# GpSimd splits the next head's weights between the low parts of the probabilities instead of ahead of them

## The chip, the cores and the metric

The kernel runs on one core of one Trainium2 chip. The metric is the device time of one launch in microseconds (us); lower is better. The core's engines are TensorE (PE; its weight loads are listed as PEld), VectorE (DVE), ScalarE (ACT), GpSimd (POOL) and SyncE (SP), which here only issues DMAs. Each engine runs its own list of instructions in order, and they wait for one another through semaphores.

## The reference, cut to what matters

The computation is two transformer blocks over 1024 tokens with width 1024. The first has three mixers side by side, of which one is a softmax attention with forget gates ("fox", 8 heads of 64), then a gated MLP. The second is a latent attention ("mla", 16 heads, 64 + 32 for queries and keys, 64 for values). Both attentions have this core for each head and each block of queries:

```
s = jnp.einsum('bqhd,bkhd->bhqk', q, k) ...          # float32 scores
s = jnp.where(mask, s, -jnp.inf)
prob = jax.nn.softmax(s, axis=-1)
outs.append(jnp.einsum('bhqk,bkhd->bqhd', prob, v))
```

ahead of which the head's q, k and v are made by matrix products with its weights.

## The kernel before, in words

**Two-part arithmetic.** Every float32 operand `a` of a product is split into `hi` (a rounded to fp32r) and `lo = a - hi`, and a product is three matmuls: hi by lo, lo by hi, hi by hi. Weights come from HBM as 173 units of 128 x 1024 (512 KB). SP loads unit u into `w_raw` as soon as unit u-2 is split (`load`, L1894). GpSimd splits it: `w_hi` (L1919, an addition of zero that rounds), then `w_lo` (L1921, a subtraction), and counts `w_split`. TensorE waits for `w_split` before it uses a unit. There are two buffers of each.

**Attention steps.** Fox and mla run the same software pipeline, one step for each head n. The first two steps are written out, the others are a loop of two. In a step TensorE first projects head n from its weights (L220), with the first two score pieces of head n-1 in the middle. Then it attends for head n-1: the scores by keys and queries are cut into 12 pieces g, of widths 512, 384, 256, 128 (g 0 to 3, first half of the queries) and 512, 512, 512, 512, 512, 384, 256, 128 (g 4 to 11, second half). In turn for each g it does:

- the value products of the high parts of piece g (`value_pe`, L622, L623; they wait for `p_hi` of g)
- the value product of the low part of piece g-1 (`value_low_pe`, L629; it waits for GpSimd's low part of g-1)
- the scores of piece g+2 (`score_pe`, L606 to L612)
- behind g 4 to 9, the score products of head n that are needed for its row maxima (`max_pe`, L652, L654, L655), in eight groups i = 0 to 7. Group 6 stands behind g = 8 and waits until DVE has reduced five groups, group 7 behind g = 9 and waits until six are reduced.

At the end of a step come nine small transposes of v (L638, L640) and one of the maxima (L660), which waits for DVE's `mx<-mx` (L717). The next step's projection stands behind it.

**ACT** makes two exponentials of each piece: `p_hi` (L668) and, in full float32, `probs` (L670). `p_hi` of g needs the low part of piece g-2 to be done, since the buffers are shared. Behind g = 6 ACT takes the logarithm and the exponential of the first half's sums (L685, L687).

**GpSimd** makes the low parts, `probs_lo = probs - p_hi` (`low_pool`, L677), 12 for a head. Its order in step n is: split the weights of head n+1 (L1919, L1921), then the 12 low parts of head n-1.

**DVE** prepares the operands of head n (in mla with L1670, `rope_x<-rope_x,rope_y`, and last L1678, `mla_q_lo<-rope_x,mla_q_hi`), reduces the maxima groups (L712), and between the fourth and the fifth of them normalizes the first half of head n-1: L698 (`newton<-ps,r`), L701 (`rec<-newton,r`), in mla also L705 (`rec<-rec,mix`), L707 (`mix<-ps,rec`). Behind the eighth it negates the maxima (L717, 128 x 8), copies v (L722, L724) and the row of maxima (L728), and normalizes the second half (L698 to L707 again). TensorE needs `mla_q_lo` of L1678 before maxima group 0.

The first step of each attention (n = 0) has no head to attend for, and behind the last step stands the attention of the last head alone. So 7 steps of fox and 15 of mla have both a split and low parts.

Of the kernel before, what the change touches and what calls it, by code (L numbers as in the profile page):

```python
# [35 lines left out]
DT = D // P  # L36
# [67 lines left out]
def build(nc, wpack, xT, pT, vecs, consts, pos, outT, f_rows):  # L104
    with ExitStack() as ctx:
# [456 lines left out]
        N_PIECES = len(PIECES)  # L562
# [80 lines left out]
        def max_pe(pe, A, n, b, i):  # L643

            q_hi, _, k_hi, _, _ = A.bufs
            r = slice(0, A.rows_max)
            bank, reduced = MAX_BANK[i]
            if reduced:
                pe.wait_ge(A.max_done, n * N_MAX + reduced)
            queries = q_hi[b][r, i * P:(i + 1) * P]  # L650
            if i >= 4:
                nc.tensor.matmul(PS[:, bank, :], queries, k_hi[b][r, 0:HALF], start=True, stop=True)  # L652
            w, c, d = max_width(i)[0], i // 4, i % 4 * P
            nc.tensor.matmul(PS[:, bank + c, 0:w], queries, k_hi[b][r, c * HALF:c * HALF + w], start=True, stop=False)  # L654
            nc.tensor.matmul(PS[:, bank + c, d:w], ident_bf[:, :], masks[:, A.mask, 0:w - d], start=False, stop=True)\  # L655
                .then_inc(A.mp_ready, 1)
# [15 lines left out]
        def low_pool(pool, A, n, g):  # L672

            off = PIECES[g][2]
            w = slice(0, HALF - off)
            pool.wait_ge(A.exp_done, n * N_PIECES + (g + 1))
            nc.gpsimd.tensor_tensor(P_lo[g % 4][:, w], Pt[g % 4][:, w], A.p_hi[g % 2][:, w].bitcast(F32), ALU.subtract)\  # L677
                .then_inc(A.p_lo_done, 1)
# [160 lines left out]
        def steps(eng, A, step):  # L839

            for b in range(2):
                step(b, b, 0)
            with eng.Fori(1, A.heads // 2) as turn:
                for b in range(2):
                    step(turn * 2 + b, b, turn)
# [144 lines left out]
        def fox_constants_pool(pool):  # L990

            pool.wait_ge(f_stored, 32)
            pool.wait_ge(rope_s, ROPE_STEPS)
            q_hi, q_lo, k_hi, k_lo, vaug = fox.bufs
            pool.wait_ge(w_split, U_FQK + 1 + 2)
            n = 0
            for b in range(2):
                for dst, value in ((q_hi[b][HD:HD + 2, :], 1.0), (q_lo[b][HD:HD + 2, :], 0.0), (k_hi[b][HD:HD + 2, :], 1.0),
                                   (k_lo[b][HD:HD + 2, :], 0.0), (vaug[b][:, :, HD:P], 1.0)):
                    nc.gpsimd.memset(dst.bitcast(F32), value).then_inc(fox.setup, 1)  # L1000
                    n += 1
                    pool.wait_ge(fox.setup, n)
# [623 lines left out]
        def mla_constants_pool(pool):  # L1626

            pool.wait_ge(unit_done, U_Z + DT + 2)
            NKV.wait(pool, "lo", 2)
            q_hi, q_lo, k_hi, k_lo, vaug = mla.bufs  # L1630
            pool.wait_ge(w_split, U_HEAD + 1 + 2)
            n = 0
            for b in range(2):
                for dst, value in ((q_lo[b][96:97, :], 0.0), (k_hi[b][96:97, :], 1.0), (k_lo[b][96:97, :], 0.0), (vaug[b][:, :, HD:P], 1.0)):
                    nc.gpsimd.memset(dst.bitcast(F32), value).then_inc(mla_constants, 1)
                    n += 1
                    pool.wait_ge(mla_constants, n)
# [247 lines left out]
        @block.sync  # L1885
        def _(sp):
            sp.dma_start(stage[:, :], consts).then_inc(consts_in, 16)
            sp.dma_start(vec[:, :], vecs).then_inc(vecs_in, 16)
            sp.wait_ge(x_in[3], 16)
            sp.dma_start(pos_i[:, :], pos).then_inc(pos_in, 16)  # L1890

            def load(u, s):
                sp.wait_ge(w_split, u + 1)
                sp.dma_start(raw[s][:, :, :].rearrange("p k n -> p (k n)"), wpack[u, :, :] if isinstance(u, int) else  # L1894
                             wpack[bass.ds(u, 1), :, :].rearrange("o p n -> (o p) n")).then_inc(w_loaded[s], 16)
            with sp.Fori(0, N_UNITS // 2) as it:
                for s in range(2):
                    load(it * 2 + s, s)
            if N_UNITS % 2:
                load(N_UNITS - 1, 0)  # L1900
            for half in range(2):
                for i in range(DT // 2):
                    N5.wait(sp, "h", half * DT + 2 * i + 2)
                    k = 2 * i
                    sp.dma_start(outT[k * P:(k + 2) * P, cols(half)].rearrange("(k p) t -> p k t", p=P), result[:, k:k + 2, cols(half)])\
                        .then_inc(out_stored, 16)
            sp.wait_ge(out_stored, 16 * DT)

        @block.gpsimd
        def _(pool):  # L1910
            pool.sem_inc(w_split, 2)
            nc.gpsimd.memset(zero[:, :], 0.0).then_inc(zero_set, 1)
            pool.wait_ge(zero_set, 1)
            no_change = zero[:, :].rearrange("p (a n) -> p a n", a=1).to_broadcast([P, DT, P])

            def split(u, s, loads, kts=slice(0, DT)):
                pool.wait_ge(w_loaded[s], loads)
                pool.wait_ge(unit_done, u + 1)
                nc.gpsimd.tensor_tensor(w_hi[s][:, kts, :], raw[s][:, kts, :], no_change[:, kts, :], ALU.add).then_inc(w_hi_done, 1)  # L1919
                pool.wait_ge(w_hi_done, u + 1)  # L1920
                nc.gpsimd.tensor_tensor(w_lo[s][:, kts, :], raw[s][:, kts, :], w_hi[s][:, kts, :].bitcast(F32), ALU.subtract)\  # L1921
                    .then_inc(w_split, 1)

            def units(first, end, kts=DT):

                k = slice(0, kts)
                with pool.Fori(0, (end - first) // 2) as it:
                    for j in range(2):
                        split(it * 2 + (first + j), (first + j) % 2, it * 16 + ((first + j) // 2 * 16 + 16), k)
                if (end - first) % 2:  # L1930
                    split(end - 1, (end - 1) % 2, (end - 1) // 2 * 16 + 16, k)

            def heads(A, first):

                def step(n, b, turn):
                    u = first + b + 1
                    split(turn * 2 + u, u % 2, turn * 16 + (u // 2 * 16 + 16))
                    if not (isinstance(n, int) and n == 0):
                        for g in range(N_PIECES):
                            low_pool(pool, A, n - 1, g)  # L1940
                steps(pool, A, step)
                for g in range(N_PIECES):
                    low_pool(pool, A, A.heads - 1, g)
            units(0, U_FQK + 1)
            fox_constants_pool(pool)
            heads(fox, U_FQK)
            units(U_FQK + FOX_H + 1, U_DN[-1])
            units(U_DN[-1], U_MIN, MLP_CHUNKS[-1])
            units(U_MIN, U_HEAD + 1)
            mla_constants_pool(pool)  # L1950
            heads(mla, U_HEAD)
            units(U_HEAD + MLA_H + 1, N_UNITS)
# [230 lines left out]
```

## Time and profile before

| what | value |
|---|---|
| median of 3 runs | 2255.83 us (2255.39 to 2258.79) |
| profiled execution | 2258.68 us, of which the profile's span is 2256.9 us |
| busy shares of the span | PE 93%, PEld 74%, DVE 49%, ACT 29%, POOL 48% |
| TensorE's mean granted clock | 0.968 of full |
| fox steps | from about 118 to 332 us, about 30.6 us each |
| mla steps | from about 1570 to 1990 us, about 27.4 and 28.0 us each in turn |

The times are microseconds from the start of the span. A step is counted here from one L717 to the next. Where the profile gives a releaser, it is the last of the things that an instruction waited for.

### The profile page before, as it was taken

To read this page: it belongs to the slowest core of one execution; us is meant where nothing else is said; L and a number is where in the kernel's file an instruction comes from. 1 tells how busy PE (TensorE), PEld (TensorE's weight loads), DVE (VectorE), ACT (ScalarE), POOL (GpSimd) and SP (SyncE) were. 2 spreads that over 40 slices of the span, in tenths; PEclk is the share of its full clock that TensorE was granted. 3 is DMA by queue.
4 is the path that set the end of the run, shared out by engine and by line. 5 is a ranking of instruction groups with operands and counts; after the bars stand their busy time and mean duration, and the time that the engine had idled before them with its cause. 6 is when DMAs were issued, how large, how long until landed. Compare 5 with 4: busy or idle time off the path is not lost.

```text
span 2256.9 us, 27160 instructions
## 1 busy us (share of the span) xinstructions
PE 2105.2 (93%) x9840; PEld 1680.7 (74%) x9840; DVE 1111.7 (49%) x1213; ACT 661.7 (29%) x1069; POOL 1090.6 (48%) x657
## 2 busy tenths in 40 slices
PE   4999999988999999999999998997999999979996
PEld 3777777877778878888878876886777777758774
DVE  6545553637541211211211278214877777763576
ACT  3334443231221000000000032112666565650322
POOL 1635544522833533634443373333666666654373
PEclk9999997998999999999999998998999999989997
DMA  3100000112211211211111121111000000001122
GB/s 141 48 20 20 19 10 19 47 38 94 93 47 51 71 56 46 75 47 46 56 56 53 49 93 47 48 46 38 20 19 19 19 19 19 19 28 47 47 72 96
DMA packets 31624, 106.98 MB, mean 47 GB/s; under 512 B 3440, under 2 KB 3632, under 8 KB 31568
## 3 DMA queue, kind: packets, MB, share of 16 engines
q1 hardware_dynamic: 27520, 96.53, 13.1%
q10 hardware_dynamic: 4048, 9.67, 1.2%
q8 instruction: 39, 0.64, 0.1%
q14 instruction: 17, 0.14, 0.0%
HBM read 101.83 MB, written 4.26 MB: 47 GB/s over the span
## 4 chain that ended last, share of the span: by engine, by line
PE 77%; DVE 15%; issue 4%; ACT 3%; POOL 1%; ACTq 0%; DVEq 0%; DMA 0%; POOLq 0%
PE ps L220 53%; PE ps L385 4%; PE ps L237 3%; PE ps L249 2%; DVE mx L712 2%; PE ps L622 2%; PE ps L607 2%; PE ps L606 2%; PE ps L608 2%; PE ps L623 1%; PE ps L629 1%; DVE h_lo L366 1%; DVE rec L705 1%; PE ps L652 1%; DVE mx L717 1%
## 5 line engine op out<-in xcount | busy, mean ns | idle before, releaser
L1919 POOL TENSOR_TENSOR w_hi<-w_raw,zero 128x1024 fp32r<-128x1024 f32 (+1 forms) x173 | 332.8, 1924 | 817.6 <-PE ps L220 578.6
L1921 POOL TENSOR_TENSOR w_lo<-w_raw,w_hi 128x1024 fp32r<-128x1024 f32 (+1 forms) x173 | 432.4, 2500 | 13.6
L220 PE MATMUL ps<-h_hi,w_lo 128*128 128x512 f32 x1328 | 335.4, 395 | 5.6 <-DVE x L512 5.1
L220 PE MATMUL ps<-h_hi,w_hi 128*128 128x512 f32 x1328 | 328.1, 389 | 0.0
L220 PE MATMUL ps<-h_lo,w_hi 128*128 128x512 f32 x1216 | 301.3, 390 | 0.0
L220 PEld LDWEIGHTS ps<-h_hi,w_lo 128*128 128x128 f32 x1328 | 249.8, 190 | 61.5 <-issue 10.6
L677 POOL TENSOR_TENSOR probs_lo<-probs,mla_p_hi 128x512 fp32r<-128x512 f32 x192 | 211.7, 1123 | 172.8 <-ACT probs L670 172.8
L220 PEld LDWEIGHTS ps<-h_hi,w_hi 128*128 128x128 f32 x1328 | 249.4, 188 | 51.6
L220 PEld LDWEIGHTS ps<-h_lo,w_hi 128*128 128x128 f32 x1216 | 229.2, 189 | 47.8
L1369 DVE TENSOR_TENSOR tmp<-ps,tmp 128x1024 f32<-128x1024 f32 x22 | 26.9, 1224 | 370.2 <-PE ps L220 363.6
L712 DVE TENSOR_REDUCE mx<-ps 128x1 f32<-128x128 f32 (+1 forms) x192 | 139.5, 754 | 75.7 <-PE ps L655 74.9
L677 POOL TENSOR_TENSOR probs_lo<-probs,fox_p_hi 128x512 fp32r<-128x512 f32 (+1 forms) x96 | 98.8, 1040 | 122.0 <-ACT probs L670 121.4
L670 ACT ACTIVATE probs<-ps 128x512 f32<-128x512 f32 (+3 forms) x288 | 140.7, 488 | 0.0
L512 DVE TENSOR_TENSOR x<-ps,x 128x1024 f32 x32 | 39.1, 1223 | 171.6 <-PE ps L220 165.1
L668 ACT ACTIVATE mla_p_hi<-ps 128x512 fp32r<-128x512 f32 x192 | 94.2, 491 | 79.2 <-PE ps L612 49.2
L1357 ACT ACTIVATE tmp<-ps 128x1024 f32<-128x1024 f32 x22 | 22.6, 1027 | 323.3 <-PE ps L220 323.2
L1359 ACT ACTIVATE a_hi<-tmp 128x1024 f32 x22 | 23.4, 1062 | 236.8 <-DVE tmp L1369 236.8
L622 PE MATMUL ps<-mla_p_hi,mla_vaug 128*128 128x512 f32 x192 | 77.5, 404 | 6.6 <-ACT mla_p_hi L668 6.5
L668 ACT ACTIVATE fox_p_hi<-ps 128x512 fp32r<-128x512 f32 (+1 forms) x96 | 46.8, 488 | 98.0 <-PE ps L612 90.1
L1371 DVE TENSOR_TENSOR a_lo<-tmp,a_hi 128x1024 f32 x22 | 59.8, 2718 | 29.4 <-ACT a_hi L1359 29.4
L606 PE MATMUL ps<-mla_q_hi,mla_k_lo 97*128 97x512 f32 x192 | 67.8, 353 | 3.3 <-DMA mla_q_hi<-c_neg 3.3
L413 DVE TENSOR_TENSOR ssq<-ssq,sq 128x512 f32<-128x512 f32 (+1 forms) x42 | 51.1, 1217 | 34.1 <-ACT sq L433 23.0
(345 smaller groups left out, 3895.0 us busy)
## 6 DMA issues: line engine op xcount, KB each, us to landing
w_raw<-in_wpack SPq DMA_DIRECT2D x173, 512.0 KB, 3.3
x<-in_xT ACTq DMA_DIRECT2D x16, 512.0 KB, 8.0
out<-result SPq DMA_DIRECT2D x8, 512.0 KB, 2.9
p_raw<-in_pT ACTq DMA_DIRECT2D x1, 1024.0 KB, 6.9
const_stage<-in_consts SPq DMA_DIRECT2D x1, 788.0 KB, 4.3
pos_i<-in_pos SPq DMA_DIRECT2D x1, 512.0 KB, 6.5
vec<-in_vecs SPq DMA_DIRECT2D x1, 284.0 KB, 5.2
mla_q_hi<-c_neg ACTq DMA_DIRECT2D x16, 4.0 KB
```

The lines of the kernel that those rows point to most:

```text
L220: last = nc.tensor.matmul(dst[:, half, :], w[slot][:, kt, :], a[:, i, t], start=(n == 0), stop=(n == total - 1))
L237: last = nc.tensor.matmul(dst[:, half, :], w[u % 2][:, kt, :], a[:, kt, t], start=(i == 0 and n == 0), stop=(i == len(order) - 1 and n == 2))
L385: last = nc.tensor.matmul(PS[:, bank, :], w[slot][:, kt, :], a[:, kt, t], start=(k == 0), stop=(k == 3 * len(order) - 1))
L606: nc.tensor.matmul(out, k_lo[b][r, keys], q_hi[b][r, t], start=True, stop=False)
L622: nc.tensor.matmul(PS[:, O_BANK[half], off:HALF], A.bufs[4][b][:, j, :], p, start=(j == 0), stop=False)
L668: nc.scalar.activation(A.p_hi[g % 2][:, 0:HALF - off], scores, ACT.Exp).then_inc(A.p_hi_done, 1)
L670: nc.scalar.activation(Pt[g % 4][:, 0:HALF - off], scores, ACT.Exp).then_inc(A.exp_done, 1)
L677: nc.gpsimd.tensor_tensor(P_lo[g % 4][:, w], Pt[g % 4][:, w], A.p_hi[g % 2][:, w].bitcast(F32), ALU.subtract)\
L712: nc.vector.reduce_max(mx[:, i:i + 1], flat(PS[:, bank:bank + 2, :])[:, 0:max_width(i)[1]] if i >= 4 else PS[:, bank, 0:max_width(i)[1]], ...
L1371: nc.vector.tensor_tensor(flat(a_lo[:, bass.ds(f, 1), :]), tmp[1][:, :], flat(a_hi[:, bass.ds(f, 1), :]).bitcast(F32), ALU.subtract).then_ ...
L1919: nc.gpsimd.tensor_tensor(w_hi[s][:, kts, :], raw[s][:, kts, :], no_change[:, kts, :], ALU.add).then_inc(w_hi_done, 1)
L1921: nc.gpsimd.tensor_tensor(w_lo[s][:, kts, :], raw[s][:, kts, :], w_hi[s][:, kts, :].bitcast(F32), ALU.subtract)\
```

## The change

In steps with low parts, GpSimd no longer splits the next head's weights first. It makes the low parts of pieces 0 to 3, then `w_hi`, then the low parts 4 to 6, then `w_lo`, then the low parts 7 to 11. The instructions are the same ones, with the same waits. Step n = 0 is as before. All else is untouched.

```diff
-            def split(u, s, loads, kts=slice(0, DT)):
+            def split_high(u, s, loads, kts=slice(0, DT)):
                 pool.wait_ge(w_loaded[s], loads)
                 pool.wait_ge(unit_done, u + 1)
                 nc.gpsimd.tensor_tensor(w_hi[s][:, kts, :], raw[s][:, kts, :], no_change[:, kts, :], ALU.add).then_inc(w_hi_done, 1)
+
+            def split_low(u, s, kts=slice(0, DT)):
                 pool.wait_ge(w_hi_done, u + 1)
                 nc.gpsimd.tensor_tensor(w_lo[s][:, kts, :], raw[s][:, kts, :], w_hi[s][:, kts, :].bitcast(F32), ALU.subtract)\
                     .then_inc(w_split, 1)
+
+            def split(u, s, loads, kts=slice(0, DT)):
+                split_high(u, s, loads, kts)
+                split_low(u, s, kts)
...
                 def step(n, b, turn):
                     u = first + b + 1
-                    split(turn * 2 + u, u % 2, turn * 16 + (u // 2 * 16 + 16))
-                    if not (isinstance(n, int) and n == 0):
-                        for g in range(N_PIECES):
-                            low_pool(pool, A, n - 1, g)
+                    loads = turn * 16 + (u // 2 * 16 + 16)
+                    if isinstance(n, int) and n == 0:
+                        split(turn * 2 + u, u % 2, loads)
+                        return
+                    for g in range(N_PIECES):
+                        low_pool(pool, A, n - 1, g)
+                        if g == 3:
+                            split_high(turn * 2 + u, u % 2, loads)
+                        if g == 6:
+                            split_low(turn * 2 + u, u % 2)
```

## Rows read from the trace of the kernel before

**Rows 1.** The page's chain that ended last, shares by engine.

```profile
PE 77%; DVE 15%; issue 4%; ACT 3%; POOL 1%; ACTq 0%; DVEq 0%; DMA 0%; POOLq 0%
```

**Rows 2.** That chain in one mla step: start us, us, what.

```profile
1757.16 0.69 DVE rec L701
...
1757.99 1.56 DVE rec L705
...
1760.19 0.82 DVE mx L712
...
1764.67 1.11 DVE mx L717
...
1765.83 0.27 PE ps L660
...
1766.31 1.84 PE ps L220 x4
```

**Rows 3.** Waits in the mla steps: total us, times, longest.

```profile
PE ps L652 <- DVE mx L712: 9.1, 15, 0.7
```

**Rows 4.** Instructions of L717 over the run, and who waited.

```profile
L717 DVE TENSOR_SCALAR mx<-mx x24: 170/1008/1127, 118.0 to 1989.6; 128x8 f32<-128x8 f32 x24
...
  PE ps L660: 15.5, 20
```

**Rows 5.** Timeline of POOL in that mla step: start, duration, line, operation.

```profile
1746.12 3.80 POOL L677 TENSOR_TENSOR probs_lo<-probs,mla_p_hi 128x512 fp32r<-128x512 f32 x4 [5.39 <-ACT probs L670]
...
1751.65 1.29 POOL L677 TENSOR_TENSOR probs_lo<-probs,mla_p_hi 128x512 fp32r<-128x512 f32 x1 [1.73 <-ACT probs L670]
...
1753.81 2.53 POOL L677 TENSOR_TENSOR probs_lo<-probs,mla_p_hi 128x512 fp32r<-128x512 f32 x2 [0.87 <-ACT probs L670]
...
1757.19 1.81 POOL L677 TENSOR_TENSOR probs_lo<-probs,mla_p_hi 128x512 fp32r<-128x512 f32 x1 [0.84 <-ACT probs L670]
...
1763.34 0.46 POOL L677 TENSOR_TENSOR probs_lo<-probs,mla_p_hi 128x128 fp32r<-128x128 f32 x1 [0.99 <-ACT probs L670]
...
1763.86 1.89 POOL L1919 TENSOR_TENSOR w_hi<-w_raw,zero 128x1024 fp32r<-128x1024 f32 x1
1765.83 2.37 POOL L1921 TENSOR_TENSOR w_lo<-w_raw,w_hi 128x1024 fp32r<-128x1024 f32 x1
```

**Rows 6.** Timeline of DVE around it.

```profile
1745.44 1.22 DVE L1670 TENSOR_TENSOR rope_x<-rope_x,rope_y 32x1024 f32<-32x1024 f32 x1
...
1750.50 1.22 DVE L1678 TENSOR_TENSOR mla_q_lo<-rope_x,mla_q_hi 32x1024 fp32r<-32x1024 f32 x1 [1.17 <-ACT mla_q_hi L1658]
...
1768.04 0.70 DVE L701 SCALAR_TENSOR_TENSOR rec<-newton,r 64x512 f32<-64x512 f32 x1
```

**Rows 7.** Timeline of ACT: p_hi of piece 6.

```profile
1753.62 0.61 ACT L668 ACTIVATE mla_p_hi<-ps 128x512 fp32r<-128x512 f32 x1
```

**Rows 8.** Timeline of PE in the same step.

```profile
1752.56 0.22 PE L654 MATMUL ps<-mla_k_hi,mla_q_hi 96*128 96x128 f32 x1
...
1753.30 0.50 PE L622 MATMUL ps<-mla_p_hi,mla_vaug 128*128 128x512 f32 x1 [0.20 <-ACT mla_p_hi L668]
...
1759.68 0.39 PE L629 MATMUL ps<-probs_lo,mla_vaug 128*128 128x512 f32 x1
```

**Rows 9.** Timeline of POOL in a fox step.

```profile
256.12 1.23 POOL L677 TENSOR_TENSOR probs_lo<-probs,fox_p_hi 128x256 fp32r<-128x256 f32 x2 [4.38 <-ACT probs L670]
...
258.94 1.28 POOL L677 TENSOR_TENSOR probs_lo<-probs,fox_p_hi 128x512 fp32r<-128x512 f32 x1 [1.58 <-ACT probs L670]
...
263.89 1.28 POOL L677 TENSOR_TENSOR probs_lo<-probs,fox_p_hi 128x512 fp32r<-128x512 f32 x1 [1.10 <-ACT probs L670]
```

**Rows 10.** Timelines of ACT, DVE and PE in that fox step.

```profile
260.34 0.60 ACT L668 ACTIVATE fox_p_hi<-ps 128x512 fp32r<-128x512 f32 x1 [0.51 <-POOL probs_lo L677]
...
264.05 1.67 DVE L701 SCALAR_TENSOR_TENSOR rec<-newton,r 64x512 f32<-64x512 f32 x1
...
266.58 0.39 PE L629 MATMUL ps<-probs_lo,fox_vaug 128*128 128x512 f32 x1
```

## The prediction

> **What bounds the kernel now.** I read the page's chain first: TensorE holds it, and DVE has a share that TensorE's busy time alone would not suggest [rows 1]. Then the chain in order of time through one mla step, to see where DVE enters. It enters twice [rows 2]. In the middle of the step the chain runs through L701, L705 and the fifth reduction L712, which releases TensorE's maxima group 6 (L652); that wait comes in each of the 15 mla steps [rows 3]. At the end it runs through L717, which releases the transpose L660, and behind that stands the next projection. GpSimd itself is hardly on the chain. So the question is what GpSimd's instructions do to these DVE instructions, and for that I laid the timelines of GpSimd and DVE side by side.
>
> **What the side-by-side reading shows.** L717 works on 128 x 8 elements. It takes 0.17 us at best and 1.01 at the median [rows 4]. In the step shown it starts at 1764.67, inside `w_hi` (1763.86 to 1765.75), and ends at 1765.78, as `w_hi` ends [rows 2, 5]. The second L701 starts inside `w_lo` (1765.83 to 1768.20) and ends at 1768.74, 0.54 us behind its end [rows 5, 6]. The first L701, ahead of the low part of piece 7, takes 0.68 us, and that low part takes 1.81 us instead of 1.29; L705 then takes 1.56 us and ends 0.55 us behind the low part's end (1759.00) [rows 2, 5]. The low part of piece 0 starts under L1670 as well [rows 5, 6]. So a DVE instruction whose inputs are all in SBUF and a GpSimd instruction exclude each other: the second waits for the first. Two figures follow: a DVE L701 or L705 that waits ends 0.55 us behind GpSimd's instruction, and a 512-wide low part that waits ends 1.15 us behind DVE's (1757.85 + 1.15 = 1759.00). L698, L707 and the reductions read PSUM, and their durations show no such wait.
>
> **What is removed.** The two split instructions leave the end of the step. Nothing of GpSimd then runs under L717, since the last low part is over by 1763.80 [rows 5]. TensorE waited 15.5 us for L717, in 20 of the 24 steps [rows 4]; the four without a wait are n = 0 and the last step of each attention, where no split follows, and L717 took 0.17 us there. These four are this change in small. With L717 at 0.17 TensorE comes to L660 with the pipeline not yet empty, some 0.07 us sooner still: 15.5 + 20 x 0.07 = 17 us saved. In steps with two small waits there (L220 follows L660 by 0.2 us of issue [rows 2]) up to 2 us more might go; I count none.
>
> **What is added, mla.** I follow the shown step. Low part 3 ends at 1746.12 + 3.80 = 1749.92 [rows 5]. `w_hi` takes 1.89: 1749.96 to 1751.85. L1678 is issued at 1750.50 and has both inputs in SBUF [rows 6]. If it waits, it ends at 1751.85 + 1.22 - 0.14 = 1752.93 instead of 1751.72 (0.14 is the overlap that L701 shows: 0.68 - 0.54). Low part 4 comes behind it: 1752.93 + 1.15 = 1754.08 instead of 1752.94. TensorE's maxima group 0, at 1752.56, slips by 0.4, of which 0.2 lies in a wait that is there anyway and most of the rest in the two groups' own pipeline; low part 4 then costs TensorE about 0.25 at its L629 [rows 8]. ACT's `p_hi` of piece 6 slips from 1753.62 to 1754.19 [rows 7], and with it `probs` of 6 and low part 6, from 1756.34 to 1756.66. `w_lo` then runs from 1756.70 to 1759.09. L701 is issued at about 1757.3 and waits: it ends at 1759.64 instead of 1757.85. Low part 7 ends at 1759.64 + 1.15 = 1760.79 instead of 1759.00, L705 at 1761.34 instead of 1759.55, and the fifth reduction at about 1762.8 instead of 1761.01: 1.8 us later. TensorE's group 6 waits for exactly this now, so the 1.8 us go to TensorE whole. Low part 7 alone would let its L629 go at 1760.84 instead of 1759.68 [rows 8], 1.2 later, which lies under the 1.8. Behind that nothing regains time, since everything to L717 follows TensorE. 15 steps x 1.8 = 27 us. Without the wait of L1678 (no row shows one behind GpSimd), `w_lo` starts 0.3 sooner and the price is 1.5: 22 us. That is the lower bound of this term; I take 1.8, since L701 and L705 show that wait for instructions of the same kind of inputs.
>
> The Trainium skill has this as a rule (SBUF — State Buffer, Who interferes with whom): a DVE instruction with two SBUF inputs contends with a GpSimd instruction that reads SBUF, and the second to issue blocks for the whole of the first. The trace agrees for L701 and L705. By the rule L1678 waits, which gives 27 us; without it 22. The page's advice to schedule whichever is off the critical path speaks against a split under L701.
>
> **What is added, fox.** The first halves have no L705, and L701 already waits for low part 7 today (1.67 us) [rows 10]. Low part 3 ends at 257.35 [rows 9], `w_hi` at 259.28, low part 4 at 260.59 instead of 260.22. `p_hi` of piece 6 slips by 0.37 [rows 10], low part 6 ends at 263.15, `w_lo` at 265.6, L701 at 266.13 instead of 265.72, and low part 7 at 267.28 instead of 265.17 [rows 9]. TensorE's L629 for it goes at 266.58 today [rows 10]; it would go at 267.35. That is 0.8 us in this step, about 0.9 in the steps of the other parity, where TensorE comes to it 0.12 sooner. 7 x 0.85 = 6 us. Without the slip of `w_hi` it is 0.4 each, 3 us.
>
> **What costs nothing.** The next head's weights would be split by about 1759.1, and its projection starts at 1766.31 [rows 2]: 7 us early, where they are now split a whole step early, at the step's start (as `w_lo` to 1768.20 is for the head after that [rows 5]). SP's load of the unit after the next is issued with it, and its data are wanted two steps on. No DMA is on the chain [rows 1]. The cover is gone only if `w_lo` slips by 7 us.
>
> **Sum.** 27 + 6 - 17 = +16 us, against the profiled execution 2258.7, so 2274.7. The median of the runs is 2.9 us below that execution, so I forecast 2255.8 + 16 = 2272 us, 0.7% slower. Its own range: 22 + 3 - 19 = +6, to 27 + 8 + 6 - 15.5 = +26, where the 8 and the 6 are bounds: fox at 1.15 a step, as if its low part 7 weren't partly covered, and 0.4 a step in mla, the slip at group 0 if the 1.8 doesn't cover it. That is 2262 to 2282.
>
> **Rivals.**
>
> *The split blocks no DVE instruction in the middle (faster).* GpSimd alone is later: low part 7 ends at about 1758.78 + 1.29 = 1760.1. L629 goes 0.4 later, and TensorE still reaches group 6 before or at 1761.05, where it waits 0.54 today. The mla cost is then nearly nothing and fox costs some 2 us: 17 - 2 = 15 us saved, 2241. It turns on one thing: whether L701 waits behind `w_lo`. Below 1.1 us for each mla step the kernel gains ((17 - 0.5) / 15). For it: the middle of a step has never had a split. Against it: the second L701 ends exactly 0.54 behind `w_lo`. Chance 0.10.
>
> *GpSimd gets in first when both wait (much slower).* At the end of `w_lo` low part 7 would run before L701, and low part 8 before L705. Each then waits a low part more, about 1.3 us: 3.1 for each mla step, 47 + 8 - 17 = +38, 2294. Against it: L705 got in ahead of low part 8, which was ready. Chance 0.05.
>
> *It cancels.* L701 is issued before `w_lo`, in many steps, and the rest of the wait is shared with the pipeline, so that a step costs about 1 us. For it: `w_lo` starts only 0.6 us ahead of L701. Against it: even then L705 would wait for `w_lo`, to about 1760.9 instead of 1759.5, 1.4 us for a step. 2252 to 2260. Chance 0.07.
>
> **How the numbers follow.** The forecast has 0.78, the three rivals 0.10, 0.05 and 0.07. A measurement of this kernel tells 0.2% (4.5 us) from no change. Slower by more: 0.78 + 0.05 and a little of the last, 0.84; within it 0.06; faster 0.10. The range that holds 8 in 10 is the forecast's own with a little of its neighbours at both ends: 2260 to 2284.
>
> **What the profile will show if this is right.** L717 at 0.17 us in all 24 steps, and no wait of L660 for it. The first L701 of mla steps at about 2.3 us, L705 at about 1.5. L1678 at about 2.4 instead of 1.22. TensorE's wait at L652 for L712 at about 2.1 us instead of 0.6, some 31 us in 15 waits. In fox a wait of L629 for `probs_lo` of about 0.8 us. The prediction is wrong if L701 keeps 0.7 us under `w_lo`, or if L652's wait grows while the steps don't.

## The result and the profile after

| | before | changed |
|---|---|---|
| median | 2255.7 us (2255.39 to 2258.79, 4 runs) | 2285.49 us (2282.88 to 2287.6, 4 runs) |
| profiled execution, and its span | 2258.68 us, 2256.9 us | 2287.6 us, 2285.8 us |
| TensorE's mean granted clock | 0.968 | 0.958 |

The changed kernel is slower: the ratio is 1.0128 with a 95% interval of 1.0111 to 1.0146, about 29 us. Slower was forecast, but by 16 us, and the range ended at 2284.

The source view of the changed kernel answers to [rows 4] and [rows 6]: count, shortest, median and longest in ns, first and last start in us (L717 over the run, the others in the mla steps).

```profile
L717 DVE TENSOR_SCALAR mx<-mx x24: 170/171/172, 117.4 to 2018.0; 128x8 f32<-128x8 f32 x24
L701 DVE SCALAR_TENSOR_TENSOR rec<-newton,r x29: 682/2007/2020, 1589.5 to 2007.8; 64x512 f32<-64x512 f32 x29
L1678 DVE TENSOR_TENSOR mla_q_lo<-rope_x,mla_q_hi x15: 2353/2372/2426, 1582.5 to 2000.9; 32x1024 fp32r<-32x1024 f32 x15
```

L717 never waits now, in all 24 steps. (In the changed kernel and those made from it `w_lo` stands at L1923, before at L1921.) L1678 takes 2.37 us instead of 1.22, and the L701 of the first half 2.01 instead of 0.68. The wait view of the mla steps (total us, times, longest) answers to [rows 3].

```profile
PE ps L652 <- DVE mx L712: 16.9, 15, 1.2
PE ps L629 <- POOL probs_lo L677: 7.7, 15, 0.5
...
PE ps L654 <- DVE mla_q_lo L1678: 2.9, 15, 0.3
```

The wait for L717 is gone from the list. Maxima group 6 waits 16.9 us instead of 9.1, and two new waits stand beside it. The timelines of one mla step of the changed kernel, the one that ends in the L717 at 1626.90, answer to [rows 2, 5, 6, 8]. First GpSimd (low parts 2 and 3; `w_hi`; low parts 4 to 6; `w_lo`; low part 7):

```profile
1609.15 1.17 POOL L677 TENSOR_TENSOR probs_lo<-probs,mla_p_hi 128x256 fp32r<-128x256 f32 x2
1610.35 1.89 POOL L1919 TENSOR_TENSOR w_hi<-w_raw,zero 128x1024 fp32r<-128x1024 f32 x1
1612.20 4.83 POOL L677 TENSOR_TENSOR probs_lo<-probs,mla_p_hi 128x512 fp32r<-128x512 f32 x3
1616.99 2.39 POOL L1923 TENSOR_TENSOR w_lo<-w_raw,w_hi 128x1024 fp32r<-128x1024 f32 x1
...
1619.35 1.72 POOL L677 TENSOR_TENSOR probs_lo<-probs,mla_p_hi 128x512 fp32r<-128x512 f32 x1
```

Then DVE:

```profile
1610.90 2.43 DVE L1678 TENSOR_TENSOR mla_q_lo<-rope_x,mla_q_hi 32x1024 fp32r<-32x1024 f32 x1 [1.17 <-ACT mla_q_hi L1658]
...
1617.91 2.02 DVE L701 SCALAR_TENSOR_TENSOR rec<-newton,r 64x512 f32<-64x512 f32 x1
1620.11 1.51 DVE L705 TENSOR_TENSOR rec<-rec,mix 64x512 f32<-64x512 f32 x1 [0.18 <-DVE rec L701]
...
1622.37 2.76 DVE L712 TENSOR_REDUCE mx<-ps 128x1 f32<-128x640 f32 x3
...
1626.90 0.17 DVE L717 TENSOR_SCALAR mx<-mx 128x8 f32<-128x8 f32 x1
```

And TensorE:

```profile
1621.12 0.50 PE L629 MATMUL ps<-probs_lo,mla_vaug 128*128 128x512 f32 x1 [0.51 <-POOL probs_lo L677]
...
1623.25 0.50 PE L652 MATMUL ps<-mla_k_hi,mla_q_hi 96*128 96x512 f32 x1 [1.19 <-DVE mx L712]
```

The chain of the forecast is there, link by link: `w_lo` ends at 1619.38, L701 0.55 us behind it at 1619.93, low part 7 at 1621.07, L705 at 1621.62, the fifth reduction releases group 6. What the forecast didn't have is in the windows view (stretch, length, busy time of each engine, the granted clock behind the busy times, DMA share and GB/s). Four rows of the changed kernel, of which the second follows on the first:

```profile
1641.00:1651.80 10.80, 9.04 (x45) 5.75 (x45) 8.54 (x11) 7.34 (x15) 10.76 (x7) 1.00 0.14 51
1651.80:1662.00 10.20, 10.20 (x39) 8.07 (x39) 6.38 (x10) 1.88 (x5) 1.53 (x3) 0.50 0.01 1
...
1774.60:1778.00 3.40, 3.40 (x15) 2.70 (x14) 1.67 (x3) 0.45 (x2) 1.12 (x2) 0.52 0.00 0
1832.70:1842.90 10.20, 10.20 (x39) 8.27 (x38) 6.53 (x10) 1.67 (x5) 1.33 (x3) 0.50 0.00 0
```

At 1651.6 TensorE comes out of the waits of 0.50 and 1.07 us at L629 and L652, and from 1651.8 to 1662.0 its granted clock is 0.50: the 1.2 GHz level, not the 2.4 of the rest. The mla steps of the changed kernel have such a stretch in every second step, seven in all, of 10.2, 3.4 or 13.7 us; each begins 0.3 to 0.7 us behind the wait at L652. The kernel before has two in these steps, of 3.4 us each, and they begin 0.8 to 0.9 us behind the wait of 0.83 us for L717 (L660). The first:

```profile
1766.60:1770.00 3.40, 3.40 (x9) 2.65 (x8) 3.16 (x6) 0.00 (x0) 1.60 (x1) 0.50 0.20 54
```

From 1600 to 1990 us the kernel before has a mean granted clock of 0.99:

```profile
1600.00:1990.00 390.00, 364.69 (x1961) 280.12 (x1960) 306.72 (x365) 233.40 (x448) 242.97 (x195) 0.99 0.06 19
```

and the changed one 0.94, with as much busy time for fewer instructions:

```profile
1600.00:1990.00 390.00, 363.34 (x1823) 270.68 (x1822) 307.38 (x339) 218.01 (x416) 237.98 (x182) 0.94 0.05 18
```

From the first L717 with a split behind it to the last, 14 mla steps apart, it is 390.8 us before (1598.8 to 1989.6) and 419.7 changed (1598.3 to 2018.0). These 28.9 us are as much as the two profiled spans differ by. Fox gains 0.9: its seven steps take 214.2 before and 213.3 changed.

### The profile page after: what moved, and what is told of

Same layout as the page of the kernel before. It is cut to its first block, busy times and chain, and to the rows that moved or that the text cites. A ratio compares the mean times of both kernels' runs of the same rounds, so it can differ in the third digit from the quotient of the medians.

```text
span 2285.8 us, 27160 instructions
## 1 busy us (share of the span) xinstructions
PE 2133.0 (93%) x9840; PEld 1690.9 (74%) x9840; DVE 1134.5 (50%) x1213; ACT 662.1 (29%) x1069; POOL 1102.6 (48%) x657
## 4 chain that ended last, share of the span: by engine, by line
PE 59%; issue 15%; POOL 14%; DVE 10%; ACT 2%; ACTq 0%; POOLq 0%; DMA 0%; DVEq 0%
PE ps L220 45%; POOL probs_lo L677 11%; PE ps L385 4%; PE ps L237 2%; PE ps L249 2%; POOL w_hi L1919 2%; POOL w_lo L1923 1%; DVE h_lo L366 1%; DVE tmp L1747 1%; DVE x L1749 1%; DVE S_all L1287 1%; DVE tmp L362 1%; DVE ssq L1835 0%; DVE result L1753 0%; DVE ssq L413 0%
## 5 line engine op out<-in xcount | busy, mean ns | idle before, releaser
L1923 POOL TENSOR_TENSOR w_lo<-w_raw,w_hi 128x1024 fp32r<-128x1024 f32 (+1 forms) x173 | 432.7, 2501 | 11.9
L677 POOL TENSOR_TENSOR probs_lo<-probs,mla_p_hi 128x512 fp32r<-128x512 f32 x192 | 225.8, 1196 | 193.5 <-ACT probs L670 192.7
L1369 DVE TENSOR_TENSOR tmp<-ps,tmp 128x1024 f32<-128x1024 f32 x22 | 26.9, 1225 | 370.3 <-PE ps L220 363.6
L629 PE MATMUL ps<-probs_lo,mla_vaug 128*128 128x512 f32 x192 | 71.7, 389 | 8.9 <-POOL probs_lo L677 8.9
```

Source lines behind the costliest of these rows:

```text
L629: nc.tensor.matmul(PS[:, O_BANK[half], off:HALF], A.bufs[4][b][:, j, :], P_lo[g % 4][:, 0:HALF - off], start=False, stop=(g in LAST_OF_HAL ...
```

## The experiments

Two theories stood. **Waits and clock**: about half of the loss is the chain of waits, the rest is the granted clock, which falls behind the longer waits in the middle of a step. **Waits alone**: the chain costs more than was worked out, and the clock is a by-product. "Mla, 14 steps" below is from the first to the last L717 of the mla steps n = 1 to 15, each in one profiled execution.

### The changed kernel with TensorE's waits filled

```diff
+        def fill_pe(count):
+            for _ in range(count):
+                nc.tensor.matmul(PS[:, O_BANK[1], 256:512], zero_bf[:, :], masks[:, 0, 0:256], start=False, stop=False)
...
+                if g == 8 and A is mla and after:
+                    fill_pe(3)
                 if g:
                     value_low_pe(pe, A, n, b, g - 1)
...
+            if i == 6 and A is mla and not (isinstance(n, int) and n == 0):
+                fill_pe(8)
             if reduced:
                 pe.wait_ge(A.max_done, n * N_MAX + reduced)
```

`zero_bf` is a 128 x 128 tile of zeros, so the small matmuls add zero.

> The changed kernel with TensorE kept busy in the two mla waits of the middle of a step: 3 small bf16 matmuls (256 columns, weights all zero, added to the open bank of the second half, so nothing changes in value) ahead of the low value product of piece 7, and 8 ahead of maxima group 6. Theory 1 (waits plus clock: about 16 us of the 29 us are the waits themselves, the other 13 to 15 us are stretches of the mla steps in which TensorE is granted half the clock after the longer gap): the half-clock stretches between 1620 and 2010 us go away or become as few as before (two of 3.4 us), and the time falls by 12 to 16 us to about 2271. Theory 2 (the waits alone: the DVE chain and the low parts cost more than worked out, the clock is a by-product): the gaps are filled but the instructions behind them start when they did; 2283 to 2288, a little above the changed kernel if anything.

Measured: 2264.17 us, 1.003 of before (1.0019 to 1.004), 21 us under the changed kernel. TensorE is given more work, and the kernel gains 21 us. The instructions of GpSimd and DVE are the changed kernel's. The windows view from 1600 to 1990:

```profile
1600.00:1990.00 390.00, 377.40 (x2060) 278.79 (x2059) 322.86 (x353) 231.83 (x441) 252.80 (x193) 1.00 0.06 18
```

The granted clock is full. Mla, 14 steps: 399.0 us (1596.5 to 1995.5) against 419.7. The waits alone would have given no gain, so that theory falls. The gain is larger than the 12 to 16 us expected. The fill itself doesn't lengthen a step: TensorE still waits 0.2 to 0.3 us behind it at each of the two places. The changed kernel shows the same without any fill: its three steps at full clock take 28.58, 28.78 and 28.75 us, the filled kernel's steps in the same places 28.50, 28.71 and 28.71, within 0.1 us of them.

### The kernel before with DVE held up, without and with the fill

```diff
             bank = MAX_BANK[i][0]
+            if i == 4 and A is mla and not (isinstance(n, int) and n == 0):
+                for k in range(2):
+                    nc.vector.reduce_max(hold[:, k:k + 1], flat(PS[:, bank:bank + 2, :])[:, 0:max_width(i)[1]], AX_X)
```

> The kernel before, with the splits at home, and DVE held up in mla steps only: the fifth reduction of the maxima is made three times (two more of about 0.8 us into a scratch column), so that TensorE waits at maxima group 6 for about 1.5 us more and nothing of GpSimd is moved. Theory 1 (waits plus clock): 15 steps x 1.5 = 23 us from the wait, and half-clock stretches appear in the mla steps as in the changed kernel, for 10 to 15 us more: 2289 to 2295. Theory 2 (waits alone): 2255.7 + 23 = about 2278, granted clock of the mla steps as before. Moving the splits would have nothing to do with the clock in either case.

Measured: 2297.08 us, 1.0184 (1.0165 to 1.0204), some 41 us above before and 2 above what was expected at most. TensorE's waits at group 6 (one line further down in this kernel) grow from 9.1 to 30.9 us, which accounts for 22:

```profile
PE ps L653 <- DVE mx L716: 30.9, 15, 2.1
```

The windows view has a clock of 0.91:

```profile
1600.00:1990.00 390.00, 357.21 (x1776) 275.34 (x1774) 292.05 (x353) 215.45 (x412) 221.50 (x178) 0.91 0.05 18
```

No split was moved, and each of the ten half-clock stretches up to 2025 us begins 0.8 to 2.0 us behind that wait. So the clock falls behind the wait in the middle of the step, whatever makes it. The fill gives the size: the same kernel with `fill_pe(20)` ahead of group 6.

> The kernel before with DVE held up by two extra reductions in each mla step, as in the run with the held-up DVE (2297), and with 20 small matmuls (256 columns, zero weights) ahead of maxima group 6, about 2.1 us, into the gap that the hold makes. Clock theory: the granted clock stays full through the mla steps, a clean mla step is 27.7 + 1.5 = 29.2 us, and the time is about 2255.7 + 23 = 2278, some 18 us under the unfilled one. Theory without the clock: the fill changes nothing, 2295 to 2300.

Measured: 2277.91 us, 1.009 (1.0073 to 1.0107), which is the forecast of 2278. The clock from 1600 to 1990 us is 0.99. Mla, 14 steps: 429.7 us held up (1595.3 to 2025.0), 411.3 with the fill (1598.5 to 2009.8). The half-clock stretches are worth 18.4 us there, and each step is 1.5 us longer than before, as the longer wait for the two reductions makes it ((30.9 - 9.1) / 15).

### Fox alone

```diff
-                        if g == 3:
+                        if g == 3 and A is fox:
                             split_high(turn * 2 + u, u % 2, loads)
-                        if g == 6:
+                        if g == 6 and A is fox:
                             split_low(turn * 2 + u, u % 2)
```

with mla's split at the head of the step, in one call ahead of the low parts.

> The change in fox steps only; the mla steps split at their head as before. Profiles: fox steps took 213.3 us in the changed kernel and 214.2 before. Theory 1: the whole loss is in mla, and fox gains some 1 to 3 us: 2253 to 2255. Theory by the prediction's terms (6 us cost, 5 us saved): 2256 to 2257. If a part of the loss came from elsewhere (the stages behind fox, or the program's code), 2260 or more.

Measured: 2254.03 us, 0.9987 (0.9978 to 0.9997). Mla, 14 steps: 390.8 us, as before. Fox, 7 steps: 211.9 us. So the whole loss is in mla, and in fox the change is a small gain, about 2 us.

### w_hi back at the head of the step

```diff
+                    split_high(turn * 2 + u, u % 2, loads)
                     for g in range(N_PIECES):
                         low_pool(pool, A, n - 1, g)
-                        if g == 3:
-                            split_high(turn * 2 + u, u % 2, loads)
                         if g == 6:
                             split_low(turn * 2 + u, u % 2)
```

> Half of the change: w_hi goes back to the head of the step, w_lo stays behind the low part of piece 6. L717 then waits for w_hi as before (1.0 us), so nothing is saved there; L701 still waits for w_lo, L1678 for nothing. By the terms: mla 15 x 1.5 = 22 us, fox about 7 x 0.3 = 2 us, no saving, about 2280 at full clock. With the clock theory the gap at group 6 also costs half-clock stretches, 8 to 15 us: 2288 to 2294. If w_lo under L701 were not the cause of the loss, the time would be near 2256.

Measured: 2297.85 us, 1.0179 (1.0162 to 1.0196), clock 0.92 from 1600 to 1990 us. The waits of its mla steps:

```profile
PE ps L652 <- DVE mx L712: 16.9, 15, 1.2
PE ps L629 <- POOL probs_lo L677: 9.0, 15, 0.6
...
PE ps L660 <- DVE mx L717: 5.2, 7, 0.7
```

The waits of the middle are 16.9 + 9.0 us, against 16.9 + 7.7 + 2.9 in the changed kernel: nearly all of them come from `w_lo` behind piece 6, and the move of `w_hi` adds 1.6 us in all. The wait for L717 is back in half of the steps, and in the others the clock is low there and hides it. The time is 4 us above what was expected at most.

### The first half's normalization behind the fifth reduction

```diff
-                if i == 3 and prev is not None:
+                if i == 4 and prev is not None:
                     norm_half_dve(dve, A, prev, 1 - b, 0, tile, gate)
```

on top of the changed kernel.

> The changed kernel with one thing moved on DVE: the first half's normalization (L698 to L707) comes behind the fifth reduction of the maxima, not ahead of it. L701 still waits for w_lo, but maxima group 6 no longer waits for L701. Theory 1 (the chain w_lo, L701, low part 7, L705, reduction 5, group 6): that wait of TensorE goes away, what is left is the late low part 7, 0.5 to 1 us for a step against 0.85 saved at L717, and few half-clock stretches: 2252 to 2262. A rival (the late low parts are what costs, DVE only rides along): the time stays above 2275.

Measured: 2271.84 us, 1.006 (1.0044 to 1.0077), between the two expectations. Group 6 no longer waits. But the normalization now stands ahead of the sixth reduction, and the wait moves to group 7 (the same line, L652):

```profile
PE ps L652 <- DVE mx L712: 19.9, 15, 1.4
```

The clock from 1600 to 1990 us is 0.96:

```profile
1600.00:1990.00 390.00, 365.67 (x1875) 270.66 (x1873) 305.90 (x347) 223.84 (x429) 241.62 (x187) 0.96 0.06 18
```

The expectation had left group 7 out, and its first theory falls with that. Nor does the run test what a late low part costs: low part 7 now follows `w_lo` at once, ahead of L701 (which waits for it instead and takes 1.3 us), and TensorE's listed waits for it at L629 are gone. The wait at group 7 isn't the work of `w_lo`: below, the same move without any split in the middle of a step has the same 19.9 us in 15 waits. It comes from the place of the normalization, so this run doesn't separate what `w_lo` adds.

### Versions with nothing in the middle

All three have both splits at the head of the step, as before. The diffs show the lines that hold them back. The first:

```diff
+                    if not (isinstance(n, int) and n == 0):
+                        pool.wait_ge(A.mx_done, n)
                     split(turn * 2 + u, u % 2, turn * 16 + (u // 2 * 16 + 16))
```

> The kernel before, with one wait more on GpSimd: from the second step on, the splits at the head of a step wait until DVE has negated the maxima of the head before (L717). Nothing runs under L717 then and nothing is put into the middle of the step. Theory 1: L717 takes 0.17 us in all 24 steps and TensorE doesn't wait for it: 17 us saved, 2239, the clock as before or better. A rival: the splits now lie wholly under DVE's second normalization and under its tail, which is late then and takes the saving back: 2250 or more.

Measured: 2243.76 us, 0.9951 (0.993 to 0.9973), between the two expectations. Fox took 208.7 us instead of 214.2, a step 0.87 less in the steps of the loop. Mla, 14 steps: 384.7 us instead of 390.8 (1590.7 to 1975.4). For mla the rival named the right places, though not the time: DVE's second L701 waits for `w_lo` (it takes 2.5 to 2.6 us), and in every second step L1678 is late for TensorE.

```profile
PE ps L654 <- DVE mla_q_lo L1678: 9.4, 7, 1.3
```

The second puts the wait later:

```diff
+                    if isinstance(n, int) and n == 1:
+                        pool.wait_ge(A.mx_done, 1)
+                    elif not isinstance(n, int):
+                        pool.wait_ge(A.norm_done, n * 2 - 2)
                     split(turn * 2 + u, u % 2, turn * 16 + (u // 2 * 16 + 16))
```

> The kernel before with the splits at the head of the step, but from the third step on they wait until DVE is through the second half's normalization (L707), a span in which DVE has only PSUM inputs to read until L1670. The splits that waited for L717 alone gained 12 us of the 17: fox steps 0.87 us each, mla steps only 0.33, where L701 then waited for w_lo and L1678 came late. Theory: here both L717 and the second L701 are free, mla steps are 27.7 - 0.85 = 26.9 us and the time is 2238 to 2241. A rival: w_lo now reaches under L1670 or the low part of piece 0 and gives some back, 2243 or more.

Measured: 2266.56 us, 1.0039 (1.0028 to 1.005). Here too the rival was right, and the clock (0.97 from 1600 to 1990) made it dearer: `w_lo` ended too late for low part 0, which then also stood behind L1670 (2.25 us instead of 1.7; L1670 itself waited for `w_lo` and took 3.0 instead of 1.2), and L629 waited for it.

```profile
PE ps L629 <- POOL probs_lo L677: 19.9, 15, 1.6
PE ps L652 <- DVE mx L712: 12.8, 15, 1.7
```

The third has one place for each, in steps with low parts, instead of the call of `split`:

```diff
+                    pool.wait_ge(A.mx_done, n)
+                    split_high(turn * 2 + u, u % 2, turn * 16 + (u // 2 * 16 + 16))
+                    if not isinstance(n, int):
+                        pool.wait_ge(A.norm_done, n * 2 - 2)
+                    split_low(turn * 2 + u, u % 2)
```

> The kernel before with both splits at the head of the step, but each behind a wait: w_hi until DVE has negated the maxima (L717), w_lo, from the third step on, until DVE is through the second half's normalization. The splits that waited for L717 alone held the second L701 for w_lo (L1678 late, mla gained 0.33 a step); those that both waited for L707 made low part 0 late (L629 waited up to 1.6 us, half-clock stretches, 2267). Theory: here neither happens, no longer gap for TensorE anywhere, L717 at 0.17 us: mla steps 26.9 us, fox steps 29.7, time 2238 to 2241. Rival: L1670 or low part 0 still meets w_lo, 2245 or more.

Measured: 2236.07 us, 0.9911 (0.9893 to 0.9928), some 20 us under before and 2 under what was expected at least. Mla, 14 steps: 376.0 us (1591.3 to 1967.3), 26.9 a step, and fox 209.5. The granted clock is 1.00 through these 14 steps: before's wait for L717 and the two half-clock stretches behind it are both gone. GpSimd and DVE in one mla step, first GpSimd (`w_hi`, `w_lo`, low parts 0 to 3), then DVE:

```profile
1752.78 1.89 POOL L1919 TENSOR_TENSOR w_hi<-w_raw,zero 128x1024 fp32r<-128x1024 f32 x1 [1.38 <-DVE mx L717]
1757.29 2.40 POOL L1923 TENSOR_TENSOR w_lo<-w_raw,w_hi 128x1024 fp32r<-128x1024 f32 x1 [2.62 <-DVE mix L707]
1760.66 3.80 POOL L677 TENSOR_TENSOR probs_lo<-probs,mla_p_hi 128x512 fp32r<-128x512 f32 x4 [0.96 <-ACT probs L670]
```

```profile
1754.98 0.68 DVE L701 SCALAR_TENSOR_TENSOR rec<-newton,r 64x512 f32<-64x512 f32 x1
1755.81 0.68 DVE L705 TENSOR_TENSOR rec<-rec,mix 64x512 f32<-64x512 f32 x1
...
1759.97 1.22 DVE L1670 TENSOR_TENSOR rope_x<-rope_x,rope_y 32x1024 f32<-32x1024 f32 x1
```

`w_hi` is over before L701, `w_lo` lies between L707 and L1670, and low part 0 isn't late.

Two more went on from it. With the first half's normalization behind the fifth reduction, as above:

> The same, and DVE normalizes the first half behind the fifth reduction, not ahead of it. It is to take away TensorE's wait of 0.54 to 0.67 us at maxima group 6, 9 us in all. Theory: part of it comes back at group 7, since the sixth reduction then stands behind the normalization: 2232 to 2240. Rival: the wait only moves to group 7 and is longer there, with half-clock stretches: 2242 or more.

Measured: 2257.55 us, 1.0001 (0.9986 to 1.0016). The rival was right: the waits at L652 grow from 9.0 to 19.9 us in all, and the clock from 1600 to 1990 is 0.96. But its last half-clock stretch in these steps ends at 1856; the steps from there to 1992 have the same waits of 1.3 and 1.4 us and the full clock (1.00). With `fill_pe(4)` ahead of group 6:

> The same as the one with two places, with 4 small matmuls (0.43 us) ahead of maxima group 6. In the kernel before there were two half-clock stretches of 3.4 us in the mla steps and one at the end, each worth 1.6 us. If the gap of 0.6 us feeds them, they go and 2 to 4 us are gained, 2235 to 2238; if they come from elsewhere, no change.

Measured: 2236.64 us, 0.9912 (0.9891 to 0.9933): no change. There was nothing to gain: the kernel without the fill has the full clock in these steps already, with waits of 0.5 to 0.7 us at group 6.

## Why the prediction was wrong, point by point

**Which way, and by which chain: right.** L717 at 0.17 us in all 24 steps, L1678 at 2.4, the first L701 at 2.0 (2.3 forecast), L705 at 1.5, TensorE's waits at L629 and L652: each was there. That L1678 waits, the step that no row showed, came out by the rule that the prediction took from the Trainium skill (SBUF — State Buffer, Who interferes with whom): it takes 2.37 us behind `w_hi` instead of 1.22.

**The mla term: right at full clock.** The filled kernel takes 399.0 us for the 14 steps. Before takes 390.8, and its two half-clock stretches of 3.4 us are worth 3.4 us together at most (half of their length). At full clock that is 399.0 - 387.4 = 11.6 us, 0.83 a step; the forecast had 1.8 - 0.85 = 0.95. The wait at L652 alone grew less than was said (16.9 us in all, not 31), since a part of it stands at L629 and at L654 ahead of it. The three together grow by 18.4 us, 1.2 a step; at least 0.45 us of a step's price of 0.83 + 0.85 stands in no listed wait of TensorE, and where it goes wasn't found.

**The fox term: mis-sized.** It was to cost 0.85 a step and cost about 0.45: in the loop a fox step takes 0.4 less than before with a saving of 0.85. TensorE's waits for low part 7 are 0.36 and 0.49 us in turn. A part of the difference is that GpSimd's next instruction starts some 0.04 us before the last one's end, where I had added a handoff to each of four. The change in fox alone gains 2 us, where these terms had a loss of 1.

**The step that failed: "at full clock", which was never written down.** The sum took every microsecond of TensorE at the clock of the rows, and of the longer wait said that "behind that nothing regains time". It didn't ask whether something behind it gets slower. Behind the pair of waits at L629 and L652 the granted clock is half in every second mla step. The filled kernel prices that at 419.7 - 399.0 = 20.7 us, less the 3.4 that before has: 17.3 us. So the 28.9 us of the 14 steps are 11.6 of waits and 17.3 of clock. That the two add up proves nothing, as both are taken against the filled kernel; what bears the division out is that the changed kernel's own full-clock steps are as long as the filled ones, that its half-clock stretches hold 52.1 us of these steps and so can cost up to 26, and that the held-up kernel gives 18.4 us in the same way. The rest of the program (fox, the first mla step, the run's own scatter) sums to about nothing.

**Could it be read beforehand?** In part. The page's clock row (the span in 40 slices of 56 us) has slices of 7 and 8 tenths, so the clock does fall in this kernel. None of them lies inside the mla steps with a split: slices 29 to 35 (1580 to 1975 us) all read 9.

```profile
PEclk9999997998999999999999998998999999989997
```

[rows 3] said that the wait that was to grow stood in every step. No row showed how much longer it could get without a price in clock. The held-up kernel is the cheap way to ask that: no split is moved in it. The Trainium skill (TensorE: Matmul & The Clock Gate, A second HAM failure mode: psum-queue depth-cycling) tells of another kernel in which short idle stretches between groups of matmuls are frequent enough to make the clock swing between its two levels. The traces agree, with a mean clock of 0.94 where waits of 0.5 and 1.1 us stand in each step. A fall of the clock was not among the rivals, and should have been.

**What stays open.** Which waits bring the clock down. The length of the wait doesn't decide it alone: in the changed kernel the stretches stand behind the waits of 1.06 or 1.07 us of every second step and never behind the 1.19 or 1.20 of the steps between, and with two places and the later normalization the same waits of 1.3 and 1.4 us are at first followed by a stretch in every second step and then by none. That the wait must be filled where it stands wasn't shown either, since the same small matmuls were never put elsewhere in the step. How the moved `w_hi` shares in the filled kernel's 0.83 us wasn't measured by itself at full clock.

## What to carry to other kernels

Ask of every SBUF-to-SBUF instruction of VectorE with two inputs which GpSimd instruction runs at that moment, and of a small `tensor_scalar` too: in these traces the one that came second waited until the other was over (L701 2.01 us instead of 0.68, L1678 2.37 instead of 1.22, L717 1.01 instead of 0.17). Long GpSimd work goes where VectorE reads PSUM or is idle, and if no gap is wide enough, its parts go to two gaps, each behind a semaphore that opens it. Where a change lengthens a wait of TensorE that comes again in every step, its price may not be the wait alone: fill the wait with matmuls that change nothing, or hold up the engine that it waits for, and read the granted clock.

## What the runs showed of the hardware that was not expected

- Giving TensorE eleven more matmuls in each mla step made the kernel 21 us faster (2285.5 to 2264.2), with the mean granted clock at 1.00 instead of 0.94 from 1600 to 1990 us.
- A held-up VectorE cost some 20 us in waits and 19 us in clock (2277.9 with the fill, 1.009 of before; 2297.1 without).
- L701 ended the same time behind the GpSimd instruction that it waited for, whichever that was: 0.55 us behind `w_lo` in the changed kernel, 0.54 behind low part 7 before in fox.
